# A weight matrix stored piece by piece, so that one transfer of 2 KB runs brings each piece

## The chip, the cores and the metric

The kernel runs on one core of a Trainium2 chip, as one program. The metric is the device time of a whole execution in microseconds; lower is better. Packing of inputs on the host before the launch isn't in it.

## The reference, cut to what matters

Two blocks of a network are computed for 256 tokens of 1024 channels. The first has a recurrent mixer and a layer that looks up rows of two tables (PEER): each token picks 16 of 16384 experts in each of 8 heads, and so uses 128 rows of table u and 128 of table v. The second block has a pooling layer and an attention layer, each followed by a gated feed-forward network (FFN) on the 256 latent tokens; the first FFN is also applied to 256 context tokens. What matters here is that FFN:

```python
def _conv_ffn(h, w_up, conv_w, conv_b, w_down):
    u = h @ w_up                       # (256, 1024) @ (1024, 5632), float32
    up = jnp.pad(u, ((0, 0), (1, 1), (0, 0)))
    u = up[:, :-2] * conv_w[0] + up[:, 1:-1] * conv_w[1] + up[:, 2:] * conv_w[2] + conv_b
    a, v = jnp.split(u, 2, axis=-1)    # columns 0..2815 and 2816..5631
    return (jax.nn.silu(a) * v) @ w_down
```

Column c of the first half is always used together with column 2816 + c of the second.

## The kernel before

All is float32. Weights stream through a ring of three slots of 128 partitions x 4096 floats (2 MB each), written by DMAs that SyncE (SP) issues in program order (`load`, L540). A load waits until the slot's last reader is done, issues its transfers, and notes the semaphore value that means "landed". `weights` (L660) makes TensorE wait for that value.

The up matrix is used in 11 pieces of 256 + 256 columns. `up` (L563) gives two transfers for a piece: for each of the 128 partitions and 8 blocks of 128 rows, 256 columns of the first half, and the same of the second half. In memory a row of the matrix is 5632 floats, so that each transfer consists of 1024 runs of 1 KB; in the slot a block's two runs lie beside each other. `down` (L568) gives one transfer a load, with runs of 512 columns, 2 KB. The 11 up pieces are loaded three times: by the loop at L605 for the context tokens (layer 0), and twice by `ffn_loads` (L617), for the latent tokens in layers 0 and 1. That makes 66 transfers.

The work around them differs:

- From about 330 to 1130 us the PEER rows are fetched. GpSimd (POOL, L2723) issues 512 indirect DMAs, *gathers*, each bringing one row of 4 KB into each of 128 partitions (0.524 MB), 256 from table u and 256 from table v, into a ring of 12 places. A gather waits until the place's last reader is done: VectorE (L1802) multiplies a u row with the tokens; TensorE multiplies v rows in pairs. The order is fixed by `ROWS` and `turns` (L379). Into TensorE's part of it `woven` (L431) sets the context work as steps: every few gathers in that order, one half step of the context's FFN (8 matmuls of 128x128 by 128x256, 16 weight loads in the trace). So TensorE meets up pieces and v rows in an order written out beforehand, and waits at whichever isn't there. Of the context's up pieces the first three are loaded from 432 us on, the others from 608 us on as the slots become free; the six down loads follow from 772 us.
- From about 1145 us the latent FFNs run. There each piece is first split into a high and a low part (ScalarE L2133, VectorE L1419), which frees its slot, and TensorE makes three passes of the parts (`mm3`). Between the two FFNs lies the attention layer.

Of the kernel before, what the change touches and what calls it, by code (L numbers as in the profile page):

```python
# [60 lines left out]
def packed_vectors(x):  # L61
    def cols(v):
        return np.reshape(v, (-1, 128)).T

    small = np.concatenate([np.reshape(x[n][0], -1) for n in
                            ("gdn_dt_bias", "gdn_a_log", "mlstm_i_bias", "mlstm_f_bias")])
    convw = np.transpose(np.reshape(x["conv_w"][0], (12, 128, 5)), (1, 0, 2)).reshape(128, 60)
    parts = [cols(x["norm1_g"][0]), cols(x["mlstm_norm_g"][0]), cols(x["gdn_norm_g"][0]), cols(x["attn_q_gain_2"][0]),
             cols(x["attn_k_gain_2"][0]), cols(x["c_2"][0]), cols(x["c_ctx_2"]),
             cols(x["pool_b_2"][0]), cols(x["pool_scale_2"][0]), cols(x["norm_w_2"]), cols(x["ada_b_2"]),  # L70
             cols(x["ffn_conv_w_2"]), cols(x["ffn_conv_b_2"]), convw, np.broadcast_to(small, (128, 32))]
    return np.ascontiguousarray(np.concatenate(parts, 1))


def packed_ada(w):

    w = np.reshape(w, (2, 4, 2, 128, 3, 4, 512))
    return np.ascontiguousarray(np.transpose(w, (0, 4, 1, 3, 2, 5, 6)).reshape(24, 128, 4096))


def packed_gates(w):

    g = np.concatenate([w[:, 2048:2064], w[:, 4112:4128]], 1)
    g = np.transpose(np.reshape(g, (8, 128, 32)), (1, 0, 2)).reshape(128, 256)
    return np.ascontiguousarray(np.concatenate([g, np.tile(np.eye(32, dtype=np.float32), (4, 1))], 1))


def packed_keys(k):
# [3 lines left out]
def program(nc, a, out):  # L92
# [32 lines left out]
    def at(name, n):  # L125

        sem = S[name]
        while name in GOES_ON:
            name, before = GOES_ON[name]
            n += before  # L130
        return sem, n

    def sb(name, n, stack=ctx, p=128):
        return stack.enter_context(nc.sbuf_tensor(name, [p, n], F32))
# [18 lines left out]
    vec = sb("vec", NVEC)  # L153
# [121 lines left out]
    bands = [(hpC[:, 392 * g:392 * g + 256], hpC[:, 392 * g + 256:392 * g + 392]) for g in range(4)]  # L275
# [208 lines left out]
    def split_done(n):  # L484

        if n in (34, 40, 41):
            return "g_lo", (34, 40, 41).index(n) + 1
        return "v_lo", n + 1 - sum(n > m for m in (34, 40, 41))
# [48 lines left out]
    def _(sp):  # L537
        free, count, nth = [None] * 4, [0] * 4, [0]

        def load(name, until, *parts, n=4, slot=None):  # L540

            i = nth[0] % n if slot is None else slot
            nth[0] += 1
            for signal in free[i] or ():
                sp.wait_ge(*at(*signal))
            for put, src in parts:
                sp.dma_start(put(slots[i]), src).then_inc(S[f"d_w{i}"], 16)
                count[i] += 16
            free[i] = until if isinstance(until, list) else [until]
            ready[name] = S[f"d_w{i}"], count[i], slots[i]  # L550
# [6 lines left out]
            return ((lambda ap: ap[:, 0:2048].rearrange("p (g c) -> p g c", g=8)),  # L557
                    a["pool_w_2"][0].rearrange("g (k p) c -> p (g k) c", p=128))

        def up_part(i):  # L560
            return lambda ap: ap.rearrange("p (k i c) -> p k i c", k=8, i=2)[:, :, i, :]

        def up(l, g):  # L563
            w = a["ffn_w_up_2"][l]
            return ((up_part(0), w[:, 256 * g:256 * g + 256].rearrange("(k p) c -> p k c", p=128)),
                    (up_part(1), w[:, 2816 + 256 * g:3072 + 256 * g].rearrange("(k p) c -> p k c", p=128)))

        def down(l, half, f0, nf):  # L568
            w = a["ffn_w_down_2"][l]
            return ((lambda ap: ap[:, 0:512 * nf].rearrange("p (f c) -> p f c", f=nf)),  # L570
                    w[128 * f0:128 * (f0 + nf), 512 * half:512 * half + 512].rearrange("(f p) c -> p f c", p=128))
# [30 lines left out]
        sp.dma_start(cl[:, 0:1536], a["c_late"]).then_inc(S["d_l"], 16)  # L602
        load("poolc", ("p_cpl", 4), pool_w(), n=3)
        for g in range(11):
            load(("cup", g), ("p_cu", 2 * g + 2), *up(0, g), n=3)  # L605
        for half in range(2):
            for q, (f0, nf) in enumerate(((0, 8), (8, 8), (16, 6))):
                load(("cdn", half, q), ("p_cd", 4 * (3 * half + q) + 4), down(0, half, f0, nf), n=3)
# [7 lines left out]

        def ffn_loads(l, n0):  # L617
            for g in range(11):
                load(("up", l, g), split_done(n0 + 2 * g + 1), *up(l, g), n=3)
            for half in range(2):  # L620
                for q, (f0, nf) in enumerate(((0, 8), (8, 8), (16, 6))):
                    load(("dn", l, half, q), split_done(n0 + 23 + 6 * half + 2 * q), down(l, half, f0, nf), n=3)

        ffn_loads(0, 0)
        load("kv", [split_done(34), split_done(35)], kcols(a["attn_w_qkv_2"][0], 1024, 512), n=3)
        for q in range(2):
            load(("q", q), split_done(37 + 2 * q), kcols(a["attn_w_qkv_2"][0], 512 * q, 512), n=3)
        for i in range(LOADS_EARLY, 24):
            load(("ada", i), ("p_adb", i - LOADS_EARLY + 1), (lambda ap: ap, a["ada"][i]), n=3)
            if i in (LOADS_EARLY + 5, 23):  # L630
                q = int(i == 23)
                load(("o", q), split_done(41 + 2 * q), kcols(a["attn_w_o_2"][0], 512 * q, 512), n=3)
        ffn_loads(1, 44)
        for n, (q, t) in enumerate(((0, 0), (0, 1), (1, 0), (1, 1))):
            sp.wait_ge(*at("a_yo" if t == 0 else "v_yo", q + 1))
# [6 lines left out]
    def _(pe):  # L642
# [509 lines left out]
        def peer():  # L1152
            for what in turns():
# [8 lines left out]
                elif what[0] == "use" and ROWS[what[1]][0] == "v" and ROWS[what[1]][2] % 2 == 1:  # L1162
                    _, s, m = ROWS[what[1]]
                    if m == 1:
                        pe.wait_ge(*at("v_wT", s + 1))
                        if s == 0:
                            for i in (5, 6):
                                pe.wait_ge(*at(held[i][0], held[i][1]))
                        elif s == 4:
                            pe.wait_ge(*at("v_add", 1))  # L1170
                    for i in range(2):
                        for k in range(m - 1, m + 1):
                            n = NTH["v", s, k]
                            q, c = four_of(k)
                            if i == 0:
                                pe.wait_ge(*at(f"d_r{n % NR}", 16 * (n // NR + 1)))
                            o = mm(vb[i][32 * q:32 * q + 32, :], alone[s % 2][:, q, c, :], ring[n % NR][:, 512 * i:512 * i + 512],
                                   s % 4 == 0 and k < 4, s % 4 == 3 and k > 27)
                            if i == 1:
                                o.then_inc(S["p_v"], 1)  # L1180
                elif what[0] == "window_sums":
                    pe.wait_ge(*at("d_l", 48))
                    for n in range(2):
                        b = take(("zb", n), "a_sz", 1)
                        for e in range(2):
                            mm(b[:, 256 * e:256 * e + 256], ones, bands[2 * n + e][0], e == 0, False)
                            k = mm(b[:, 256 * e + 120:256 * e + 256], ones, bands[2 * n + e][1], False, e == 1)
                    k.then_inc(S["p_zb"], 1)
# [215 lines left out]
    def _(ve):  # L1404
# [357 lines left out]
        def rows(t, step):  # L1762


            y, r = yrows[:, t, :], ss[:, 4 * t + 2:4 * t + 3]
            _, r2, root, s, rs = norm_at(t)
            if step == 0:
                ve.wait_ge(*at("d_g2", 32))
                told(tt(y, x1[:, t, :], nfb, MUL), *rows_at(t, "gain"))
            elif step == 1:  # L1770
                ve.wait_ge(*at("a_ss", 5 + 2 * t))
                seq(ve.reciprocal(r, ss[:, 4 * t + 1:4 * t + 2]))
                told(stt(r2, r, 1.0 / 1024, r, MUL, MUL), *rows_at(t, "root"))
            else:
                ve.wait_ge(*at("a_ss", 6 + 2 * t))
                if t == 0:
                    ve.wait_ge(*at("p_ckv", 3))
                seq(ve.reciprocal(s, root))
                seq(tt(rs, r, s, MUL))
                told(ts(zrows[:, t, :], y, rs, None, MUL, BYP), *rows_at(t, "pool"))  # L1780
                told(ts(y, y, r, None, MUL, BYP), *rows_at(t, "scaled"))

        def peer():
            for what in turns():
# [9 lines left out]
                elif what[0] == "use" and ROWS[what[1]][0] == "u":  # L1794
                    n = what[1]
                    _, t, m = ROWS[n]
                    j, k = 8 * t + m // 16, m % 16
                    if j > 1 and k == 0:
# [851 lines left out]
    def _(po):  # L2650
# [115 lines left out]


_INS = ["x", "w_in", "w_out", "norm2_g", "normf_g", "peer_wq", "peer_u", "peer_v", "ctx_2", "pool_w_2", "attn_w_qkv_2",
        "attn_w_o_2", "ffn_w_up_2", "ffn_w_down_2"]


# [19 lines left out]
```

## Time and profile before

| what | value |
|---|---|
| median of 3 runs | 1712.83 us (1711.22 to 1714.83) |
| the profiled execution | 1713.59 us, span of its instructions 1711.7 us |
| TensorE busy | 88% of the span, mean granted clock 0.94 |
| VectorE, GpSimd, ScalarE busy | 64%, 46%, 32% |
| moved by DMA | 477.24 MB, mean 279 GB/s |
| of these by q0, the gathers | 268.47 MB |
| of these by q1, what SP issues | 207.27 MB |

How to read it: times of stretches are microseconds from the span's start. A line such as L666 is a helper that issues every matmul; tiles tell the groups apart. `ps` is a PSUM bank, `wring` the slots, `arena` the memory that the tables' rows and the activations share, and a few gathers land in the fourth slot and so carry the name `wring` too. PEld is TensorE's loading of weights, which shows best when a matmul started. q0 is the queue of GpSimd's gathers, q1 that of SP's loads; the share in a queue's row is the time of its packets over the 16 DMA engines. That can be over 100% in sum, since packets overlap, so that a share near 1.03 means that the DMA engines had always something to do.

### The profile page before, as it was taken

How to read it: one execution, taken by the hardware profiler on the slowest of the kernel's cores; microseconds unless marked ns; L12 is line 12 of the kernel's file. 1: busy time of each engine (PE TensorE's matmuls, PEld its weight loads, DVE VectorE, ACT ScalarE, POOL GpSimd, SP SyncE). 2: the span in 40 equal slices, each digit the busy share in tenths (PEclk: the TensorE clock that was granted, in tenths of full speed). 3: DMA queues.
4: the chain of work that ended last, by engine and by line, in shares of the span. 5: the costliest groups of instructions: out<-in, count | busy, mean ns of one | idle time of the engine just before them, and what ended most of it. 6: DMA issues, size and time to landing. Idle time of an engine off the chain costs nothing.

```text
span 1711.7 us, 23479 instructions
## 1 busy us (share of the span) xinstructions
PE 1498.0 (88%) x9034; PEld 1109.4 (65%) x9034; DVE 1093.5 (64%) x2121; ACT 554.4 (32%) x782; POOL 790.4 (46%) x746
## 2 busy tenths in 40 slices
PE   7999998775566699999788866989999999999999
PEld 6997676663212266666333432449999985699999
DVE  4865654689489867766856665237775436567753
ACT  6652121211221131322100011236654524466542
POOL 0024230276667765746777777624561101225630
PEclk9999999997878899999999997999999898999999
DMA  7447770498999999999999999985654425746550
GB/s 273 149 148 294 278 278 25 158 398 305 384 398 400 409 396 391 394 382 400 406 404 400 404 371 408 408 307 187 195 185 158 175 105 191 266 130 196 192 178 26
DMA packets 188575, 477.24 MB, mean 279 GB/s; under 512 B 10544, under 2 KB 80432, under 8 KB 185264
## 3 DMA queue, kind: packets, MB, share of 16 engines
q0 software_dynamic: 73728, 268.47, 40.3%
q1 hardware_dynamic: 114736, 207.27, 34.1%
q8 instruction: 72, 1.18, 0.3%
q14 instruction: 39, 0.32, 0.1%
HBM read 474.65 MB, written 1.05 MB: 278 GB/s over the span
## 4 chain that ended last, share of the span: by engine, by line
PE 57%; DMA 15%; DVE 10%; POOL 7%; issue 4%; ACT 1%; DVEq 0%; ACTq 0%; SPq 0%; POOLq 0%
PE ps L666 57%; DMA arena<-in_peer_v,cl 8%; POOL arena L2723 6%; DMA wring<-in_ffn_w_up 3%; DVE arena L1802 2%; DMA wring<-in_peer_v,cl 2%; DVE arena L1419 1%; POOL wring L2723 1%; DMA arena<-in_peer_u,arena 1%; PE ps L670 1%; DVE arena L1425 1%; DMA wring<-in_peer_u,arena 1%; DVE wring L1802 1%; DVE arena L1732 0%; DMA wring<-in_ada 0%
## 5 line engine op out<-in xcount | busy, mean ns | idle before, releaser
L666 PE MATMUL ps<-arena,wring 128*128 128x256 f32 (+2 forms) x2360 | 595.5, 489 | 105.5 <-DMA arena<-in_peer_v,cl 97.4
L666 PEld LDWEIGHTS ps<-arena,wring 128*128 128x128 f32 (+1 forms) x2360 | 330.4, 167 | 352.7 <-DMA arena<-in_peer_v,cl 176.5
L1802 DVE CUSTOM_DVE_ANT_0 arena<-arena 128x1024 f32<-128x1024 f32 x214 | 257.2, 1227 | 124.7 <-DMA arena<-in_peer_u,arena 121.3
L2723 POOL DMA_INDIRECT arena<-in_peer_u,arena x214 | 240.2, 1123 | 198.5 <-DVE arena L1760 80.0
L2723 POOL DMA_INDIRECT arena<-in_peer_v,cl x214 | 222.9, 1042 | 82.4 <-issue 57.9
L2130 ACT ACT_TABLE_LOAD x64 | 82.1, 1283 | 388.1 <-DVE arena L1802 266.9
L1419 DVE TENSOR_TENSOR wl<-wring,wh 128x2048 fp32r<-128x2048 f32 (+1 forms) x76 | 167.8, 2208 | 60.7 <-ACT wh L2133 58.6
L666 PE MATMUL ps<-hh,wh 128*128 128x256 f32 x704 | 201.2, 286 | 3.9 <-DVE hl L1425 3.9
L666 PE MATMUL ps<-hl,wh 128*128 128x256 f32 x704 | 200.8, 285 | 0.0
L666 PE MATMUL ps<-hh,wl 128*128 128x256 f32 x704 | 200.7, 285 | 0.0
L1425 DVE SCALAR_TENSOR_TENSOR cvb<-ps,vec,cvb 128x255 f32<-128x255 f32 x264 | 127.5, 483 | 106.9 <-ACT cvb L2130 99.6
L2133 ACT ACTIVATE wh<-wring 128x2048 fp32r<-128x2048 f32 x78 | 146.1, 1873 | 76.5 <-PE ps L666 74.7
L2741 POOL TENSOR_TENSOR cvb<-cvb 128x256 f32<-128x256 f32 x44 | 97.2, 2210 | 106.5 <-ACT cvb L2130 106.5
L666 PEld LDWEIGHTS ps<-arena 128*128 128x128 f32 (+1 forms) x868 | 103.7, 193 | 56.1 <-issue 28.6
L666 PEld LDWEIGHTS ps<-hh,wh 128*128 128x128 f32 x704 | 136.8, 194 | 4.3 <-issue 4.3
L666 PEld LDWEIGHTS ps<-hl,wh 128*128 128x128 f32 x704 | 136.9, 194 | 0.0
L666 PEld LDWEIGHTS ps<-hh,wl 128*128 128x128 f32 x704 | 136.8, 194 | 0.0
L666 PE MATMUL ps<-arena 128*128 128x128 f32 (+4 forms) x868 | 117.0, 294 | 19.7 <-ACT arena L2133 10.8
L2130 ACT ACTIVATE cvb<-ps,vec 128x256 f32<-128x256 f32 x132 | 74.6, 565 | 178.2 <-PE ps L666 174.5
L2677 POOL TENSOR_TENSOR arena<-arena,cl 128x256 f32<-128x256 f32 x56 | 43.0, 768 | 167.4 <-PE ps L666 164.2
L666 PE MATMUL ps<-ah,wh 128*128 128x256 f32 x352 | 99.6, 283 | 0.0
L666 PE MATMUL ps<-al,wh 128*128 128x256 f32 x352 | 99.6, 283 | 0.0
(261 smaller groups left out, 2324.0 us busy)
## 6 DMA issues: line engine op xcount, KB each, us to landing
wring<-in_ffn_w_up SPq DMA_DIRECT2D x66, 1024.0 KB, 8.3
wring<-in_ada SPq DMA_DIRECT2D x24, 2048.0 KB, 8.7
wring<-in_ffn_w_down SPq DMA_DIRECT2D x12, 2048.0 KB, 8.4
wring<-in_w_in SPq DMA_DIRECT2D x8, 2048.0 KB, 8.1
wring<-in_ffn_w_down SPq DMA_DIRECT2D x6, 1536.0 KB, 7.9
wring<-in_peer_wq SPq DMA_DIRECT2D x4, 2048.0 KB, 20.7
wring<-in_attn_w_qkv SPq DMA_DIRECT2D x4, 2048.0 KB, 9.0
wring<-in_w_out SPq DMA_DIRECT2D x2, 2048.0 KB, 8.2
```

Source lines behind the costliest of these rows:

```text
L666: return pe.matmul(o, l, r, start=start, stop=stop)
L670: return pe.transpose(o, i, ident[0:n, 0:n])
L1419: return ve.tensor_tensor(o, x, y, op)
L1425: return ve.scalar_tensor_tensor(o, x, s, y, op0, op1)
L1802: ve.tensor_tensor_reduce(out=o, in0=o, in1=h2[:, t, :], scale=1.0, scalar=0.0, op0=MUL, op1=ADD, accum_out=dots[j % 2][:, k:k + 1]).then_ ...
L2130: return ac.activation(o, x, f, bias=bias, scale=scale, accum_out=accum)
L2133: return ac.activation(o, x, ACT.Copy)
L2677: k = po.tensor_tensor(OTs[l % 2][:, m:m + 2, :], AM[:, m:m + 2, :], bc(cl[:, o:o + 128], 2, 1), MUL)
L2723: po.indirect_dma_start(out=ring[n % NR], out_offset=None, in_=table, in_offset=bass.IndirectOffsetOnAxis(ap=which, axis=0)).then_inc(S[f" ...
L2741: seq(po.tensor_tensor(cv[:, 0, :], cv[:, 0, :], cv[:, 1, :], MUL))
```

## The change

The host packs the up matrices of both layers into a new input, `ups`, of shape (2 layers, 11 pieces, 8 blocks, 128 rows, 512): a row of a piece has its 256 columns of the first half and its 256 of the second beside each other. A load is one transfer from it, with 1024 runs of 2 KB, and raises its semaphore by 16 where the pair raised it by 32. What lies in the slot is the same as before; order, slots and waits are the same too. A piece is one region of 2 MB in memory: partitions 2 KB apart, blocks 256 KB apart.

```diff
+def packed_up(w):
+
+    return np.ascontiguousarray(np.transpose(np.reshape(w, (2, 8, 128, 2, 11, 256)), (0, 4, 1, 2, 3, 5)).reshape(2, 11, 8, 128, 512))
...
-        def up_part(i):
-            return lambda ap: ap.rearrange("p (k i c) -> p k i c", k=8, i=2)[:, :, i, :]
-
         def up(l, g):
-            w = a["ffn_w_up_2"][l]
-            return ((up_part(0), w[:, 256 * g:256 * g + 256].rearrange("(k p) c -> p k c", p=128)),
-                    (up_part(1), w[:, 2816 + 256 * g:3072 + 256 * g].rearrange("(k p) c -> p k c", p=128)))
+            return (lambda ap: ap.rearrange("p (k x) -> p k x", k=8)), a["ups"][l, g].rearrange("k p x -> p k x")
...
-            load(("cup", g), ("p_cu", 2 * g + 2), *up(0, g), n=3)
+            load(("cup", g), ("p_cu", 2 * g + 2), up(0, g), n=3)
...
-                load(("up", l, g), split_done(n0 + 2 * g + 1), *up(l, g), n=3)
+                load(("up", l, g), split_done(n0 + 2 * g + 1), up(l, g), n=3)
```

The input `ffn_w_up_2` is no longer passed to the chip.

## Rows read from the trace of the kernel before

**Rows 1.** The page's parts 1, 3 and 6: engines, DMA queues, the matrix's loads

```profile
PE 1498.0 (88%) x9034; PEld 1109.4 (65%) x9034; DVE 1093.5 (64%) x2121; ACT 554.4 (32%) x782; POOL 790.4 (46%) x746
...
wring<-in_ffn_w_up SPq DMA_DIRECT2D x66, 1024.0 KB, 8.3
```

**Rows 2.** The table by stretches: us, busy (x) by engine, PEclk, DMA share, GB/s

```profile
596.00:725.00 129.00, 128.45 (x581) 87.31 (x579) 97.94 (x233) 31.58 (x53) 84.09 (x78) 1.00 1.04 394
...
733.00:736.00 3.00, 3.00 (x8) 2.37 (x7) 1.71 (x4) 0.00 (x0) 0.00 (x0) 0.50 1.04 396
...
825.00:975.00 150.00, 128.50 (x483) 63.42 (x483) 99.11 (x239) 9.55 (x15) 111.46 (x104) 0.97 1.03 405
975.00:1025.00 50.00, 37.94 (x147) 18.60 (x146) 35.21 (x86) 4.17 (x6) 39.11 (x36) 0.95 0.99 374
1160.00:1350.00 190.00, 189.84 (x1570) 189.87 (x1571) 120.17 (x135) 106.05 (x117) 81.47 (x71) 0.99 0.55 184
```

**Rows 3.** The chain that ended last, 590 to 830: start us, us, what

```profile
596.28 90.09 PE ps L666 x400
...
686.79 44.34 DMA wring<-in_ffn_w_up
```

**Rows 4.** Waits of PE, 596 to 811: us, times, longest

```profile
PE ps L666 <- DMA wring<-in_ffn_w_up: 6.3, 1, 6.3
```

**Rows 5.** PEld in order of time, 720 to 760: start us, us

```profile
721.19 3.32 PEld L666 LDWEIGHTS ps<-arena,wring 128*128 128x128 f32 x16 [0.84 <-issue]
731.18 6.03 PEld L666 LDWEIGHTS ps<-arena,wring 128*128 128x128 f32 x16 [6.67 <-DMA wring<-in_ffn_w_up]
737.54 0.14 PEld L666 LDWEIGHTS ps<-arena,wring 128*32 128x32 f32 x4 [0.33 <-issue]
...
744.87 6.77 PEld L666 LDWEIGHTS ps<-arena,wring 128*128 128x128 f32 x32 [0.84 <-issue]
751.97 0.14 PEld L666 LDWEIGHTS ps<-arena,wring 128*32 128x32 f32 x4 [0.33 <-issue]
```

**Rows 6.** POOL's gathers that waited for PE, in order of time

```profile
625.22 0.94 POOL L2723 DMA_INDIRECT wring<-in_peer_u,arena  x1 [2.67 <-PE ps L666]
...
639.66 0.94 POOL L2723 DMA_INDIRECT arena<-in_peer_u,arena  x1 [2.55 <-PE ps L666]
...
740.22 0.94 POOL L2723 DMA_INDIRECT arena<-in_peer_u,arena  x1 [9.44 <-PE ps L666]
```

**Rows 7.** DMA from 465 to 485, gathers beside 1 KB runs: packets, MB, share

```profile
q0 software_dynamic: 1701, 6.19, 79.5%
q1 hardware_dynamic: 1704, 1.71, 24.4%
```

**Rows 8.** DMA from 560 to 590, gathers alone

```profile
q0 software_dynamic: 3375, 12.29, 102.9%
```

**Rows 9.** DMA from 856 to 868, gathers beside 2 KB runs (w_down)

```profile
q0 software_dynamic: 806, 2.94, 62.4%
q1 hardware_dynamic: 913, 1.87, 41.0%
```

**Rows 10.** DMA from 731 to 757, all queues

```profile
DMA packets 5356, 9.81 MB, mean 377 GB/s; under 512 B 249, under 2 KB 3869, under 8 KB 5355
```

**Rows 11.** DMA issues, 686 to 688, then 772 to 773: KB, us to landing

```profile
wring<-in_ffn_w_up SPq DMA_DIRECT2D x2, 1024.0 KB, 38.1
...
wring<-in_ffn_w_down SPq DMA_DIRECT2D x1, 2048.0 KB, 24.4
```

**Rows 12.** Waits of POOL, 825 to 1050

```profile
POOL arena L2723 <- PE ps L666: 7.1, 14, 1.4
POOL wring L2723 <- PE ps L666: 6.9, 4, 3.3
```

**Rows 13.** DMA from 596 to 686, then from 825 to 975, the q1 rows

```profile
q1 hardware_dynamic: 7297, 7.36, 23.5%
...
q1 hardware_dynamic: 2864, 5.77, 10.2%
```

More of the change, by code:

```diff
@@ L2768 @@
 _INS = ["x", "w_in", "w_out", "norm2_g", "normf_g", "peer_wq", "peer_u", "peer_v", "ctx_2", "pool_w_2", "attn_w_qkv_2",
-        "attn_w_o_2", "ffn_w_up_2", "ffn_w_down_2"]
+        "attn_w_o_2", "ffn_w_down_2"]
 def kernel(**inputs):
@@ L2780 @@
     given = {n: x[n] for n in _INS}
-    given |= {"ada": packed_ada(x["ada_w_2"]), "c_base": base, "c_levels": levels, "c_late": late, "c_bands": bands, "vec": packed_vectors(x),
+    given |= {"ups": packed_up(x["ffn_w_up_2"]), "ada": packed_ada(x["ada_w_2"]), "c_base": base, "c_levels": levels, "c_late": late, "c_bands": bands, "vec": packed_vectors(x),
               "gates": packed_gates(x["w_in"][0]), "keys": packed_keys(x["peer_keys"][0])}
```

## The prediction

> **What bounds the kernel now.** I read the page first: 66 transfers of 1 MB from the up matrix [rows 1]. TensorE is busy for 88% of the span, but that is a mean over stages, so the table by stretches comes next [rows 2]. Two thirds of the up loads feed the latent FFNs. From 1160 to 1350 TensorE is busy for 189.84 of 190 us at clock 0.99 and the DMA engines for 55%: loads are hidden there. The other third, 11 pieces, feeds the context's FFN beside the gathers. From 596 to 725 TensorE is busy for 128.45 of 129 us and DMA's share is 1.04, at 394 GB/s: both are full. From 825 on DMA is full too (405 GB/s), but for 975 to 1025 (374 GB/s). The chain of waits says what gives way [rows 3]: TensorE's work for 90.09 us, then a load of an up piece, 44.34 us long, then TensorE again. In TensorE's waits this load is the only DMA that it waits for between 596 and 811, 6.3 us once [rows 4].
>
> **What that stall costs.** In TensorE's weight loads a whole step is 16 + 16 loads in 6.77 us, and the v rows behind it begin 7.10 us after its start (744.87 to 751.97). The step cut in two by the stall starts at 721.19, and its v rows at 737.54, so 16.35 us later [rows 5]. The stall costs 16.35 - 7.10 = 9.25 us, and not 6.3: behind the wait 16 weight loads take 6.03 us, before it 3.32. The table shows why: the granted clock is 0.50 from 733 to 736, the lower level of 1.2 GHz, after TensorE has idled [rows 2].
>
> **Why the load was late.** GpSimd, held back by TensorE, issues eight gathers in 639.66 - 625.22 = 14.44 us [rows 6], 1.8 us each. The order sets a step every 5.6 gathers (L431), two steps for a piece: 11.2 gathers, 20.2 us. So at TensorE's pace gathers need 8 x 0.524 / 14.44 = 290 GB/s, and a piece of 2.10 MB has to come every 20.2 us, 104 GB/s: 394 in all.
> With 1 KB runs beside gathers, q1 moves 1.71 MB in 20 us, 85.5 GB/s, and q0 6.19 MB, 309.5 GB/s [rows 7]. The two queues take about as many packets each (1704 and 1701), so bytes go by packet size. A piece takes 2.10 / 85.5 = 24.5 us, over 4 us more than the period. Each load falls further behind, to a median of 38.1 us to landing for the two transfers issued at 686 [rows 11], and the last of it at 731.1 [rows 3].
>
> **The change, part by part.**
> *Packets of 2 KB beside gathers.* The down loads show them: from 856 to 868 q1 moves 1.87 MB in 12 us, 156 GB/s, and q0 2.94 MB, 245 GB/s [rows 9]. A piece takes 2.10 / 156 = 13.5 us. That is under 20.2 us, so no backlog builds up; a piece may take 44.3 - 6.3 = 38 us from its issue before TensorE misses it [rows 3, 4]. A down load issued at 772, in the same mix and with TensorE still busy, took 24.4 us [rows 11]. I take the stall as gone: -9.25 us on TensorE's chain.
> *Gathers get less while a load runs.* 245 GB/s for 13.5 us and 410 (12.29 MB in 30 us [rows 8]) for the other 6.7 us make a mean of 300, against 290 needed. That just suffices.
> *DMA's own work.* While a 1 KB piece loads, gathers lose (410 - 309.5) / 410 of 24.5 us, 6.0 us; while a 2 KB piece loads, (410 - 245) / 410 of 13.5 us, 5.4 us. The saving is 0.59 us a piece, for 11 pieces 6.5 us. The packets' own time gives a lower value: 0.235 x 16 x 90 us / 7297 = 46.4 ns for 1 KB, 0.102 x 16 x 150 / 2864 = 85.5 ns for 2 KB [rows 13]; 7.3 ns a pair, for 11264 pairs over 16 engines 5.1 us.
> The Trainium skill (DMA: Bandwidth & Descriptors, "Why small descriptors are slow (HBM only)") speaks against this: a packet costs 3 cycles on top of one for each 32 bytes, and joining is said to pay only up to 256 bytes. By that, two packets of 32 + 3 cycles become one of 64 + 3, 4.3% less, and this term would be about 2.8 us, an estimate from that page. The trace has a larger effect, 8% (92.8 to 85.5 ns), and the sum goes by the trace.
> *Three early pieces* are loaded between 432 and 558 us, beside gathers that TensorE waits for. Their share of the saving, 3 x 0.59 = 1.8 us, comes before 596 and adds to the 9.25.
> *Issues.* 33 fewer transfers for SP. SP waits for slots, and nothing is queued behind a load but the next one. In the context's stage a pair's second issue is held up by the backlog, and that ends with it. I cost it at nothing; what it is worth is in the stall.
> *The 22 latent pieces.* They are hidden by TensorE (DMA share 0.55, above): nothing. Without that cover they would bring a gain too, since the same bytes come sooner. At 1124 the first two are issued behind the last gathers, pool_w's 1 MB ahead of them; ScalarE reads the first at 1146. Nothing again; taking share from the last few gathers could cost 1 us at most.
>
> **The sum.** TensorE's chain gives 9.25 + 1.8 = 11.0 us by 811. Whether this arrives at 1125 depends on DMA: it was full all the while, so the total of its work can't end earlier than that work shrinks. That is 6.5 us, and the gap behind the stall, where GpSimd had nothing to issue for 9.44 us [rows 6] and DMA fell to 377 GB/s for 26 us [rows 10], 18 under the 395 of 1 KB runs beside gathers [rows 7]: 26 x 18 / 395 = 1.2 us. So DMA's bound is 7.7 us. GpSimd bounds it as well: from 825 to 1050 it waits for TensorE's release 18 times, 14.0 us in all [rows 12]; the rest is its own pace, which passes the whole 11.0 on, as does the stretch at 374 GB/s, where DMA could catch up by 50 x (1 - 374/410) = 4.4 us. Between 7.7 and 11.0 I take 7.7, because 825 to 975 runs at 405 GB/s, next to the 410 of gathers alone. The profiled execution took 1713.59 us, 0.76 over the median: 1705.9 for it, 1705.1 against the median of 1712.83. A measurement of this kernel can tell about 0.2%, 3.4 us, from no change.
>
> **The rivals.**
> *The whole chain arrives* (18%). DMA keeps up and catches up at 975 to 1025; the gain is 11.0, the time 1701.8. For it: GpSimd hardly waits in that stretch. Against: the DMA rate there.
> *The wait only moves* (17%). Packets of the new matrix cost as much a byte as before, because all 16 engines read one region of 2 MB with blocks 256 KB apart, which no row shows. The down matrix, with its own regular rows, speaks against it. Then DMA's bound leaves the 1.2 us of the gap: 1711.6. TensorE waits for a v row instead of a piece.
> *Slower* (8%). Gathers fall from 309.5 to 245 GB/s while a load runs, and 12 places are used up in 12 x 0.524 / 245 = 25.7 us, where TensorE's pace asks for 12 x 1.8 = 21.7. A stretch of two loads end to end makes TensorE wait for a v row, up to 4 us, and each wait is followed by a half step at the lower clock, 2.7 us. That is 6.7 us for each; from two such waits on, the gain is gone, and three of them give 1712.8 - 7.7 + 20 = 1725. Against it: the two down loads at 772 and 791 are 20 us apart beside busy TensorE, and no wait for a gather stands in TensorE's waits before 811 [rows 4].
> *The runs stay at 1 KB* (2%), if the transfer is cut otherwise than the down loads: 1712.8.
>
> **How the numbers follow.** The forecast has the remaining 55%, with its own range from 5.1 us (the packets' own time, the gap not closed) to 11.0: 1701.8 to 1707.7. The range takes in the whole-chain case with 1.8 us more, should the clock of other stretches gain too: 1700.0. Upward it takes in most of the case of the moved wait: 1711.8. Outside stay the slower case and its like. Faster by over 0.2% (below 1709.4): 55 + 18, and a third of the moved-wait case, 78%. Within: 14%. Slower: 8%.
>
> **What would show it.** In the changed trace the up loads are 33 transfers of 2048 KB; beside gathers q1 runs near 156 GB/s and q0 near 245; landing falls from 38 to 15 to 25 us; PE has no wait for an up piece between 596 and 811, PEclk stays at 1.00 there, and this stretch ends 9 to 11 us earlier. At 1125 the shift is still 7 to 11 us, and after 1160 it doesn't change. I am wrong if PE waits for v rows there instead, if q1's 2 KB packets take over 90 ns, or if the shift at 811 shrinks below 3 us by 1125.

## The result, and the profile after

The changed kernel takes 1710.37 us, the kernel before 1714.84 us on the same chip (medians of 20 runs each). The ratio is 0.998, with a 95% interval of 0.9971 to 0.9990, so 1.7 to 5.0 us less. The difference of the medians is 4.5 us, and the ratio itself stands for 3.4. Three more measurements of the same changed kernel, told below, gave 0.9962, 0.9963 and 0.9974. Weighted by the inverse squares of their intervals' widths the four make 0.9975, 4.3 us. The forecast was a gain of 7.7 us. The sign came; of the size this measurement's ratio gives under half (3.4 us), the four together a little over half.

The page's parts 1, 3 and 6 of the changed kernel; its profiled execution took 1709.29 us, 4.30 less than that of before:

```profile
span 1707.4 us, 23446 instructions
...
PE 1502.6 (88%) x9034; PEld 1113.6 (65%) x9034; DVE 1093.1 (64%) x2121; ACT 554.4 (32%) x782; POOL 797.2 (47%) x746
...
wring<-in_ups SPq DMA_DIRECT2D x33, 2048.0 KB, 10.7
```

33 transfers of 2048 KB stand where [rows 1] had 66 of 1024 KB. No engine's busy time falls by more than 0.4 us: the gain is in waiting. The table by stretches, columns as in [rows 2]:

```profile
596.00:725.00 129.00, 128.99 (x587) 86.40 (x586) 97.31 (x231) 31.58 (x53) 82.19 (x76) 1.00 1.02 398
...
730.00:745.00 15.00, 15.00 (x68) 10.20 (x68) 13.83 (x38) 2.07 (x4) 8.87 (x9) 1.00 1.03 402
...
825.00:975.00 150.00, 129.13 (x481) 63.24 (x481) 98.25 (x234) 9.55 (x15) 107.92 (x102) 0.94 1.03 404
975.00:1025.00 50.00, 35.07 (x135) 16.50 (x134) 33.76 (x85) 5.09 (x6) 39.28 (x36) 0.91 1.00 389
```

The clock of 0.50 is gone, and so is the stall. TensorE's waits for other engines and DMAs from 596 to 811 (us, times, longest), against [rows 4]:

```profile
PE ps L666 <- DMA arena<-in_peer_v,cl: 2.2, 2, 1.2
```

TensorE's weight loads in order of time (start us, us), against [rows 5]:

```profile
719.25 3.32 PEld L666 LDWEIGHTS ps<-arena,wring 128*128 128x128 f32 x16 [0.84 <-issue]
...
724.75 6.77 PEld L666 LDWEIGHTS ps<-arena,wring 128*128 128x128 f32 x32 [0.84 <-issue]
731.85 0.14 PEld L666 LDWEIGHTS ps<-arena,wring 128*32 128x32 f32 x4 [0.33 <-issue]
```

The step takes 6.77 us with its v rows 7.10 us after its start, the undisturbed value. The two queues from 618 to 624, beside each other in the stage that mattered (packets, MB, share):

```profile
q0 software_dynamic: 426, 1.56, 64.5%
q1 hardware_dynamic: 429, 0.88, 38.1%
```

That is 260 GB/s for the gathers and 147 for the load; 245 and 156 were forecast from [rows 9]. Taken over a whole load the rate is lower: the packets of one piece spread over 14.9 to 16.4 us of the trace, 128 to 141 GB/s, where 13.5 us were forecast. The five up loads issued between 604 and 700 land after a median of 19.7 us; ten transfers of before took 32.4 in the same window.

So the stall and the load behind it went as forecast, at somewhat lower rates. One sign failed in this profile already: the stretch was to end 9 to 11 us earlier, and gather 288, issued near its end, comes 5.5 us earlier (below). The rest of what didn't come is seen in the chain that ended last (start us, us, what), against [rows 3]:

```profile
599.83 102.50 PE ps L666 x464
...
702.44 7.79 PE ps L666 x32
...
710.57 81.49 PE ps L666 x366
...
803.12 15.74 DMA arena<-in_peer_v,cl
...
826.75 11.84 DMA arena<-in_peer_v,cl
```

TensorE's work now runs from 599.83 to 792, and then the chain passes to gathers of v rows. The gathers issued from 768 to 792 (KB left out by the view; the last number is us to landing), first in the kernel before:

```profile
arena<-in_peer_u,arena POOLq DMA_INDIRECT x8, 8.8
arena<-in_peer_v,cl POOLq DMA_INDIRECT x3, 9.3
```

and in the changed kernel:

```profile
arena<-in_peer_u,arena POOLq DMA_INDIRECT x6, 15.4
arena<-in_peer_v,cl POOLq DMA_INDIRECT x6, 15.6
```

The stall had held up GpSimd too ([rows 6]), and so DMA's queue of gathers had run short. Without the stall it is nearly twice as long in time (15.4 and 15.6 us to landing against 8.8 and 9.3). Waits for gathers from 785 to 870 (us, times, longest), before:

```profile
PEld ps L666 <- DMA arena<-in_peer_v,cl: 9.1, 6, 3.6
...
DVE arena L1802 <- DMA arena<-in_peer_u,arena: 7.2, 5, 2.3
```

after:

```profile
DVE arena L1802 <- DMA arena<-in_peer_u,arena: 16.5, 10, 5.8
...
PEld ps L666 <- DMA arena<-in_peer_v,cl: 14.6, 10, 3.6
```

**Progress by gather.** To see what is given back, the kernels have to be compared at the same point of the work, not at the same time. The 512 gathers are issued in one fixed order, so the time between the issues of gather m and gather n, counted from 0, is such a ruler. It is worked out from GpSimd's instructions in each profiled execution. The three early up loads fall in 64 to 144, the stall of before in 208 to 288.

```
kernel (runs of the context's up loads)  64-96  64-144  208-288  288-368
before (1 KB)                             48.8   125.8    147.1    121.0
changed kernel (2 KB)                     52.9   127.6    138.1    124.6
```

The stall's 9.0 us are there, and 3.6 of them are gone again 80 gathers later. At gather 208 the changed kernel is 3.5 us behind (661.3 against 657.8), at 288 5.5 ahead, at 368 1.9 ahead, at 511 3.7 ahead (1121.6 against 1125.3). The experiments' tables lean on the columns above, which agree within 2 to 5 us among kernels of a kind; from 64 to 208 the spread is larger (224.7 to 230.2 us in the four kernels with early runs of 1 KB). From 368 to 511 the time goes with the chip more than with the kernel: 197.6 to 200.6 us in the five profiles from chips where the kernel before takes 1713 to 1715 us, 205.4 to 213.2 in the twelve from chips where it takes 1725 to 1727, with DMA at 396 to 402 GB/s in three of the first and 385 to 390 in three of the others. Effects of 3 to 4 us can't be followed through that stretch across chips.

### The profile page after: what moved, and what is told of

It is laid out like the page before. It is cut to its first block, busy times and chain, and to the rows that moved or that the text cites. A ratio compares the mean times of both kernels' runs of the same rounds, so it can differ in the third digit from the quotient of the medians.

```text
span 1707.4 us, 23446 instructions
## 1 busy us (share of the span) xinstructions
PE 1502.6 (88%) x9034; PEld 1113.6 (65%) x9034; DVE 1093.1 (64%) x2121; ACT 554.4 (32%) x782; POOL 797.2 (47%) x746
## 4 chain that ended last, share of the span: by engine, by line
PE 59%; DMA 12%; DVE 9%; POOL 9%; issue 4%; ACT 1%; DVEq 0%; ACTq 0%; POOLq 0%
PE ps L666 59%; DMA arena<-in_peer_v,cl 9%; POOL arena L2723 7%; DVE arena L1802 2%; DMA wring<-in_peer_v,cl 2%; POOL wring L2723 1%; DVE arena L1419 1%; DVE arena L1425 1%; PE ps L670 1%; DMA wring<-in_peer_u,arena 1%; DMA wring<-in_ada 1%; DVE wring L1802 0%; DVE arena L1732 0%; DVE pr L1422 0%; DVE arena L1422 0%
## 5 line engine op out<-in xcount | busy, mean ns | idle before, releaser
L666 PE MATMUL ps<-arena,wring 128*128 128x256 f32 (+2 forms) x2360 | 600.1, 491 | 103.2 <-DMA arena<-in_peer_v,cl 97.7
L666 PEld LDWEIGHTS ps<-arena,wring 128*128 128x128 f32 (+1 forms) x2360 | 332.0, 167 | 352.6 <-DMA arena<-in_peer_v,cl 175.5
L2723 POOL DMA_INDIRECT arena<-in_peer_u,arena x214 | 240.8, 1125 | 190.9 <-DVE arena L1760 79.3
L2723 POOL DMA_INDIRECT arena<-in_peer_v,cl x214 | 226.7, 1059 | 78.9 <-issue 58.2
L666 PE MATMUL ps<-hh,wh 128*128 128x256 f32 x704 | 202.1, 287 | 3.9 <-DVE hl L1425 3.9
L666 PE MATMUL ps<-hl,wh 128*128 128x256 f32 x704 | 201.6, 286 | 0.0
L666 PE MATMUL ps<-hh,wl 128*128 128x256 f32 x704 | 201.6, 286 | 0.0
L666 PEld LDWEIGHTS ps<-hh,wh 128*128 128x128 f32 x704 | 137.7, 196 | 4.4 <-issue 4.4
L666 PEld LDWEIGHTS ps<-arena 128*128 128x128 f32 (+1 forms) x868 | 103.7, 193 | 56.1 <-issue 28.6
L666 PEld LDWEIGHTS ps<-hl,wh 128*128 128x128 f32 x704 | 137.8, 196 | 0.0
L666 PEld LDWEIGHTS ps<-hh,wl 128*128 128x128 f32 x704 | 137.7, 196 | 0.0
L666 PE MATMUL ps<-arena 128*128 128x128 f32 (+4 forms) x868 | 117.0, 294 | 19.7 <-ACT arena L2133 10.8
L666 PE MATMUL ps<-ah,wh 128*128 128x256 f32 x352 | 99.6, 283 | 0.0
L666 PE MATMUL ps<-ah,wl 128*128 128x256 f32 x352 | 99.6, 283 | 0.0
## 6 DMA issues: line engine op xcount, KB each, us to landing
wring<-in_peer_wq SPq DMA_DIRECT2D x4, 2048.0 KB, 14.6
```

The costliest lines, as they stand in the source:

```text
L666: return pe.matmul(o, l, r, start=start, stop=stop)
L2723: po.indirect_dma_start(out=ring[n % NR], out_offset=None, in_=table, in_offset=bass.IndirectOffsetOnAxis(ap=which, axis=0)).then_inc(S[f" ...
```

## The experiments

Four questions: which of the 33 loads matter; whether it is the runs or the layout in memory; whether DMA's work takes the rest of the gain back; and what becomes of the three early pieces. Where it stands, `up_old` is the pair of transfers of before, from the matrix of before. Medians are compared with the kernel before on the same chip. An edit moves the line numbers: L674, L671 and L668 below are the matmul helper that was L666.

### The changed kernel again

No edit.

> The changed kernel once more, for a second profile. Theory A (DMA takes back what TensorE gains): the stretch at TensorE's pace ends about 9 us sooner after its own start than before, and 3 to 5 us of that are given back before 860, as waits of TensorE and VectorE for gathers; in all 3 to 5 us faster than before. Theory B (the profile taken was an unlucky one): the 9 us are kept to 1125, in all 8 to 11 us faster. The slow patch of DMA at 515 to 535 returns if it belongs to the change, and is elsewhere or absent if it doesn't.

1720.18 against 1725.07 us, ratio 0.9962 (0.9942 to 0.9983). This chip is 10 us slower for both kernels; only ratios and differences go from one chip to another. By the ruler it repeats the stall's end and the give-back, 138.1 us from 208 to 288 and 126.8 from 288 to 368 (first of the three repeats in the table of the early pieces).

### New loads for the context alone

```diff
-                load(("up", l, g), split_done(n0 + 2 * g + 1), up(l, g), n=3)
+                load(("up", l, g), split_done(n0 + 2 * g + 1), *up_old(l, g), n=3)
```

> Only the context's 11 pieces come from the packed matrix in 2 KB runs, the 22 latent pieces as before. Both theories: as the changed kernel, 0.998 of before within 0.001 (3 to 5 us faster), because the latent FFNs hide their loads. If the latent pieces had a part: closer to 1.

1722.36 us, 0.9981 (0.9957 to 1.0005). By the ruler it is the changed kernel: 138.5 us from 208 to 288, 123.9 from 288 to 368. The only DMAs that TensorE waits for from 596 to 811 are v rows:

```profile
PE ps L674 <- DMA arena<-in_peer_v,cl: 2.2, 2, 1.2
```

### New loads for the latent FFNs alone

```diff
-            load(("cup", g), ("p_cu", 2 * g + 2), up(0, g), n=3)
+            load(("cup", g), ("p_cu", 2 * g + 2), *up_old(0, g), n=3)
```

> Only the 22 latent pieces come from the packed matrix, the context's as before. Theory A and B: no difference, within 1 us of before, and the stall of some 6 us for a context piece near 725 is back. A rival, that the latent stages or the last gathers at 1125 pay for or gain from the larger packets: 2 us or more either way.

1723.97 us, 0.9988 (0.9968 to 1.0007), nothing that can be told from none. The stall is back, 146.8 us from 208 to 288; TensorE's waits for DMAs from 596 to 830:

```profile
PE ps L674 <- DMA wring<-in_ffn_w_up: 7.2, 2, 6.4
```

With the run for the context alone, this places the gain in the context's 11 loads as far as the profiles go. The two ratios differ by less than their intervals and don't show it by themselves.

### The new layout with runs of 1 KB

```diff
+        def up_halves(l, g):
+            def part(i):
+                return lambda ap: ap.rearrange("p (k i c) -> p k i c", k=8, i=2)[:, :, i, :]
+            return tuple((part(i), a["ups"][l, g][:, :, 256 * i:256 * i + 256].rearrange("k p x -> p k x")) for i in range(2))
...
-            load(("cup", g), ("p_cu", 2 * g + 2), up(0, g), n=3)
+            load(("cup", g), ("p_cu", 2 * g + 2), *up_halves(0, g), n=3)
...
-                load(("up", l, g), split_done(n0 + 2 * g + 1), up(l, g), n=3)
+                load(("up", l, g), split_done(n0 + 2 * g + 1), *up_halves(l, g), n=3)
```

> The packed matrix, but each piece in two transfers with runs of 1 KB, as before: layout in memory alone. If the length of the run is the cause (A and B): as before, within 1 us, q1 near 85 GB/s beside gathers, the stall near 725 there. If the nearness of the data in memory is the cause: the gain of the changed kernel, 3 to 5 us.

1726.22 us, 1.0002 (0.9979 to 1.0024). The queues from 465 to 485 are those of [rows 7], and TensorE's wait from 596 to 830 is the old one:

```profile
q0 software_dynamic: 1700, 6.19, 79.6%
q1 hardware_dynamic: 1698, 1.71, 24.3%
```

```profile
PE ps L671 <- DMA wring<-in_ups: 6.1, 2, 4.6
```

Where the bytes lie in memory does nothing that can be measured here. The stall goes with the length of the runs. This run also has 66 transfers again, as the kernel before had; no run separates their number from the length of their runs in time. For the rates the trace does: the down loads of before are single transfers with 2 KB runs and had 156 GB/s, and the same 33 transfers with longer runs, below, have 210 and 353.

### Half the bytes in the late loads

This run leaves out half of the up matrix's rows for the context's pieces from the fourth on; the matmuls are all still done.

```diff
-            load(("cup", g), ("p_cu", 2 * g + 2), up(0, g), n=3)
+            load(("cup", g), ("p_cu", 2 * g + 2), up(0, g) if g < 3 else
+                 ((lambda ap: ap[:, 0:2048].rearrange("p (k x) -> p k x", k=4)), a["ups"][0, g, 0:4].rearrange("k p x -> p k x")), n=3)
```

> The changed kernel, but of the last eight context pieces only the first four of eight blocks are loaded (the other half of a slot keeps old numbers, so the context's values are others). This takes about 8 x 2.7 = 21 us of work from DMA, from 612 us on. Theory A (TensorE's pace bounds the stage, the changed kernel then gives back about 5 us because its gathers land later): the stage ends 9 us sooner as in the changed kernel, hardly anything is given back, and the whole is 8 to 12 us faster than before, 0.993 to 0.995. Theory C (DMA's work bounds the whole stretch from 596 to 1125): about 20 us or more beyond the changed kernel, 0.986 or less.

1717.38 against 1727.25 us, 0.9953 (0.9931 to 0.9974): 8.1 us less than before (4.5 to 11.9), where the changed kernel has 4.3 less. The intervals of the two overlap, so that this difference rests on the ruler more than on the times. From 208 to 288 it takes 137.9 us, like the changed kernel. From 288 to 368 it takes 119.0, where six profiles with late runs of 2 KB took 122.5 to 126.8: nothing is given back, in one profile. That speaks for DMA's work as what takes the gain back. 8.4 MB fewer would be 21 us at 400 GB/s, and only some 4 us of them reach the end; without the debt another pace is the bound, as the forecast had it with TensorE's chain. The table from 596 to 811 shows DMA no longer pressed, 373 GB/s:

```profile
596.00:811.00 215.00, 206.98 (x944) 139.55 (x936) 162.84 (x390) 55.72 (x93) 139.51 (x128) 0.99 0.99 373
```

### New loads for the three early pieces alone, and for the eight late ones alone

```diff
-            load(("cup", g), ("p_cu", 2 * g + 2), up(0, g), n=3)
+            load(("cup", g), ("p_cu", 2 * g + 2), *((up(0, g),) if g < 3 else up_old(0, g)), n=3)
```

The second kernel has `g > 2` in place of `g < 3`; both keep `up_old` for the latent FFNs.

> Only the three context pieces loaded between 432 and 558 us come in 2 KB runs, all others as before. The prediction gave them 1.8 us. Theory A: nothing (1.000 within the interval), since GpSimd's pace between 505 and 545 takes the lead away: DMA falls to 300 to 360 GB/s there and gather 128 is issued at the same time as in the kernel before, within 1.5 us. The stall near 725 stays.

> Only the context's last eight pieces come in 2 KB runs. Theory A: the whole effect of the change, 3 to 6 us (0.9965 to 0.998), with no load stall between 596 and 811. If the early three carry part of it: less than the changed kernel by 2 us.

Early: 1725.73 us, 1.0010 (0.9989 to 1.0031). Late: 1721.07 us, 0.9970 (0.9947 to 0.9994). The eight late pieces carry the gain. Waits of TensorE from 596 to 815 in the first,

```profile
PE ps L674 <- DMA wring<-in_ffn_w_up: 5.2, 2, 4.3
```

and in the second:

```profile
PE ps L674 <- DMA arena<-in_peer_v,cl: 2.3, 3, 1.1
```

The early pieces show in the first column of the ruler:

```
kernel                        64-96  64-144  208-288  288-368
new latent loads alone (1 KB)  48.6   128.6    146.8    122.1
new layout, 1 KB runs          48.0   127.2    146.8    121.0
late eight new (early 1 KB)    47.8   126.9    137.5    125.6
early three new (late 1 KB)    52.8   128.3    144.2    123.7
context alone new (2 KB)       52.2   129.1    138.5    123.9
changed kernel, three repeats  52.3   126.5    138.1    126.8
                               53.6   126.5    139.5    122.5
                               53.4   129.8    137.3    126.0
```

With early runs of 2 KB gather 96 comes 4 to 5 us later: the loads take from the gathers, at a time when the loads are in no hurry and the gathers are. By gather 144 this is made up: 125.8 to 128.6 us with 1 KB, 126.5 to 129.8 with 2 KB. So the saved DMA work isn't lost to another load, it is just not used. From 510 to 540, before and then after:

```profile
510.00:540.00 30.00, 21.35 (x67) 6.36 (x65) 28.93 (x66) 1.50 (x2) 23.00 (x20) 0.94 1.03 404
```

```profile
510.00:540.00 30.00, 17.32 (x55) 6.37 (x55) 28.93 (x65) 1.42 (x2) 24.52 (x19) 0.81 0.94 351
```

VectorE is busy for 28.93 of 30 us in both. GpSimd is full as well: 19 gathers take it 24.52 us, each issue follows the one before after 0.30 us, and some issues take 1.99 us that take 0.94 elsewhere. The chain that ended last runs over it in the changed kernel:

```profile
512.54 1.99 POOL arena L2723
...
536.17 1.99 POOL arena L2723
```

So the pace of GpSimd and VectorE is the bound there, and not DMA, which falls to 351 GB/s; which of the two engines sets it, no run separates. The ruler says the same more broadly: from gather 112 to 144 all 17 profiles took 47.2 to 50.8 us, whether DMA moved 362 GB/s meanwhile or 412. Nor is the drop a mark of the new loads by itself: with early runs of 1 KB the stretch from 510 to 540 had 356 to 404 GB/s, with 2 KB 333 to 363.

### Longer runs: 4 KB and 16 KB

Two, or all eight, of a piece's blocks are packed beside each other for each partition. Here is the kernel with 16 KB; the other has 4 and 2 for 1 and 8.

```diff
-... .reshape(2, 11, 8, 128, 512))
+... .reshape(2, 11, 1, 8, 128, 512).transpose(0, 1, 2, 4, 3, 5).reshape(2, 11, 1, 128, 4096))
...
-            return (lambda ap: ap.rearrange("p (k x) -> p k x", k=8)), a["ups"][l, g].rearrange("k p x -> p k x")
+            return (lambda ap: ap.rearrange("p (k x) -> p k x", k=1)), a["ups"][l, g].rearrange("k p x -> p k x")
```

> All pieces in runs of 4 KB (two blocks beside each other in memory), the slot as before. Packets as large as the gathers' own: beside gathers q1 and q0 should each get about 200 GB/s, a piece takes 10 to 11 us, and DMA's work for a piece falls from 5.4 to about 5.1 us. Theory A: no wait for a load, debt to gathers 2 us smaller than in the changed kernel, 0 to 3 us faster than it. A rival: gathers with half the rate for 10 us make TensorE wait within the stage, and it is slower than the changed kernel.

> All pieces in runs of 16 KB, one for each partition. If DMA takes turns by packet, q1 gets about 320 GB/s beside gathers and q0 some 80 while a piece loads (7 us), unless a packet is cut. Theory A: gathers landing 5 us later each time, made good within the period, so as the changed kernel within 3 us; a rival, that such a hole of 7 us makes TensorE wait for a v row at each of the eight pieces, each followed by the lower clock: 10 us or more slower than before.

4 KB: 1721.78 us, 0.9981 (0.9958 to 1.0004). 16 KB: 1719.56 us, 0.9963 (0.9940 to 0.9987). Neither can be told from the changed kernel (0.9963 on the chip of the 16 KB run; it was not run on that of the 4 KB run). The queues, for 4 KB from 620 to 624, and for 16 KB from 641 to 644:

```profile
q0 software_dynamic: 228, 0.84, 51.5%
q1 hardware_dynamic: 206, 0.84, 51.2%
```

```profile
q1 hardware_dynamic: 65, 1.06, 83.7%
q0 software_dynamic: 60, 0.22, 18.1%
```

In the middle of a load the queues take about as many packets each at every length: 1704 to 1701 at 1 KB, 429 to 426 at 2 KB, 206 to 228 at 4 KB, 65 to 60 at 16 KB. So the load's rate beside gathers is 85.5, 147, 210 and 353 GB/s at 1, 2, 4 and 16 KB. The Trainium skill (DMA: Bandwidth & Descriptors, "Queues, rings and completion order") states that each DMA engine takes turns between its queues packet by packet, a packet being some 9 to 17 descriptors. The equal counts here agree with turns of equally many runs; how many runs make a turn they don't show. At 16 KB gathers keep 73 GB/s, and gather 96 is 8 us later than with 1 KB (56.2 us); but a late load is over sooner (its packets spread over 6.3 to 8.2 us of the trace, and behind the middle of a load gathers get more than one packet for one), and its one profile took 118.6 us from 288 to 368, as with half the bytes. With 4 KB one profile kept only some 3.5 us up to gather 368 (142.1 + 122.5 against 268.2), less than with 2 KB, so that single profiles don't put the lengths in order. The time at the end shows no more of this than its interval of 4 us lets through.

### The early loads spread out

If early loads hurt by pressing on the gathers all at once, they should be spaced. The first three wait until TensorE has used 32, 40 and 56 of the 256 gathers of v rows. It is tried with 2 KB runs, with the kernel before (1 KB), and with 16 KB runs.

```diff
+            if g < 3:
+                sp.wait_ge(*at("p_v", (32, 40, 56)[g]))
```

> The changed kernel, but its first three context pieces are issued later: after 32, 40 and 56 of the v rows are used (about 508, 526 and 577 us) instead of at 432. Theory A: the early loads in 2 KB runs take rate from gathers that TensorE and VectorE wait for (gather 96 was issued some 4 us later than with 1 KB runs), and DMA then stands partly idle at 515 to 540; issued there, they are nearly free. Gather 96 is issued 5 us or more sooner than in the changed kernel, and the whole is 2 to 6 us faster than it. A rival, that the stretch up to 596 is bound by the pace of GpSimd and VectorE anyway: gather 96 is sooner, gather 144 and the end aren't, within 1 us.

> The kernel before with the same delay of the first three context pieces. Their loads then take 24 us each beside gathers; the third is issued at 577 and has some 45 us. Theory A: 0 to 4 us faster than before; the stall of a later piece stays, and could come sooner since all eight others queue behind.

> The changed kernel for a third time, beside the staggered one on the same chip. Theory A: 0.996 to 0.998 of before; from gather 208 to gather 368 some 5 us less than in the kernel before, of 9 us less from 208 to 288.

One chip: spaced with 2 KB 1717.18 us, 0.9953 (0.9934 to 0.9973); the kernel before, spaced, 1722.12 us, 0.9990 (0.9971 to 1.0010); the changed kernel 1719.73 us, 0.9963 (0.9943 to 0.9984).

> Runs of 16 KB for all pieces, and the first three context pieces delayed to 32, 40 and 56 used v rows. If the two effects are separate (the early loads' timing, worth 7 us up to gather 144; and DMA's debt after the stage, 6 us less with 16 KB runs from gather 208 to 368), they add up: 0.990 to 0.994 of before, 4 us or more faster than the staggered kernel with 2 KB runs. If what is saved early is lost at the next stretch that GpSimd and VectorE bound: as the staggered kernel within 2 us.

> The staggered kernel with 2 KB runs again, for a closer figure: 0.994 to 0.9965 of before; from gather 64 to gather 144 about 7 us less than in the changed kernel.

> The changed kernel a fourth time on the chip of the two others: 0.9965 to 0.998, so 2 to 5 us slower than the staggered one if the 7 us are partly kept.

Another chip: spaced with 16 KB 1704.81 us, 0.9933 (0.9913 to 0.9952); with 2 KB 1707.73 us, 0.9957 (0.9941 to 0.9973); the changed kernel 1711.67 us, 0.9974 (0.9957 to 0.9991).

```
kernel                          64-96  64-144  208-288  288-368
before, spaced (1 KB)            46.8   118.9    149.5    122.2
spaced, 2 KB, first chip         46.1   119.9    142.2    121.5
spaced, 2 KB, second chip        45.4   120.1    139.3    126.7
spaced, 16 KB                    45.0   118.3    137.9    122.1
half the bytes (late, 2 KB)      53.2   129.0    137.9    119.0
4 KB                             56.0   129.6    142.1    122.5
16 KB                            56.2   129.0    137.9    118.6
```

Spacing wins some 8 to 11 us up to gather 144, in all four profiles that have it (118.3 to 120.1, where 125.8 to 129.8 stood without). The kernel before keeps none of it that can be measured: its stall is still there (7.7 us of waits from 596 to 815) and grows from 147 to 149.5 us.

```profile
PE ps L668 <- DMA wring<-in_ffn_w_up: 7.7, 3, 4.4
```

With 2 KB runs, where the only DMAs waited for in that window are v rows,

```profile
PE ps L668 <- DMA arena<-in_peer_v,cl: 1.6, 2, 1.0
```

a part arrives: the ratio is lower than the changed kernel's by 0.0010 on one chip and 0.0017 on the other, 2 to 3 us, which the intervals don't separate. With 16 KB runs the end is 11.5 us earlier than the kernel before by the ratio (0.67% of 1715.11) and 10.3 by the medians, the best of all that ran; it is clear of the changed kernel beside it (0.9974, 0.9957 to 0.9991), but not of the spaced one with 2 KB, from which 4 us or more were expected and 2.9 came by the medians. Its rows from 505 to 540 and from 596 to 811,

```profile
505.00:540.00 35.00, 22.12 (x64) 6.48 (x58) 33.02 (x78) 4.87 (x6) 28.01 (x22) 0.78 1.02 412
...
596.00:811.00 215.00, 207.72 (x934) 139.40 (x935) 163.88 (x390) 55.68 (x93) 130.78 (x124) 0.99 1.02 409
```

beside the changed kernel's from 505 to 540:

```profile
505.00:540.00 35.00, 22.32 (x77) 9.02 (x76) 33.65 (x76) 1.42 (x2) 27.74 (x21) 0.83 0.95 359
```

DMA moves 412 GB/s where it moved 359, because loads lie where GpSimd and VectorE are the bound, and then 409 GB/s over the full stage. The reading is that spacing uses DMA's spare time and long runs cut its work behind. That both parts are needed isn't shown: spacing alone and 16 KB alone were each within their intervals of the changed kernel.

## Why the prediction was right, and where it was wrong

The mechanism came, and its size was wrong. The sum had 7.7 us, made of 6.5 us of DMA's saved work for 11 pieces and 1.2 us for the gap behind the stall; about 4.3 arrived. The term that failed for certain is the share of the three early pieces, 3 x 0.59 = 1.8 us of the 6.5; whether the other 1.2 us came stays open.

**The stall: right.** "The stall costs 16.35 - 7.10 = 9.25 us" and is gone. From 208 to 288 the four kernels with late runs of 1 KB and no spacing took 146.2 us on average (before, new latent loads alone, new layout, early three), the six with 2 KB 138.2 (the changed kernel four times, context alone, late eight): 8.0 us less. The new layout with 1 KB runs keeps the stall, so that the layout isn't what removes it.

**DMA's bound on the late pieces: right, as far as the profiles tell.** From 288 to 368 the same kernels take 122.0 and 124.9 us, so 2.9 of the 8.0 us are given back and 5.1 are kept. The forecast's step for this is 0.59 us of DMA work saved a piece; for the eight late pieces 4.7. That it comes so near 5.1 is partly luck: with the changed kernel's own rates, 147 and 260 GB/s, the same step gives 6.0 - 5.2 = 0.8 us a piece and 6.3 for eight, and the packets' own time (46.4 and 85.8 ns) gives 3.6. Half the bytes, which lifts that bound, kept 11.3 us to gather 368 (137.9 + 119.0 against 146.2 + 122.0), in one profile, and the forecast had 9.25 to 11.0 for TensorE's chain alone. The Trainium skill's 4.3% a pair ("Why small descriptors are slow (HBM only)" in DMA: Bandwidth & Descriptors) would have saved 2.8 / 11 = 0.25 us a piece, an estimate from that page, 2.0 for eight. The trace doesn't agree: a 2 KB packet took 0.241 x 16 x 90 / 4047 = 85.8 ns in the changed kernel from 596 to 686, in the row below, against 46.4 for 1 KB [rows 13], 7.5% less than two of those.

```profile
q1 hardware_dynamic: 4047, 8.18, 24.1%
```

**The three early pieces: wrong.** The step that failed is the one that took the saving of 0.59 us for all 11 pieces, and with it "Their share of the saving, 3 x 0.59 = 1.8 us, comes before 596 and adds to the 9.25". Measured: 1.0010 (0.9989 to 1.0031) for those three alone, and 0.9970 for the eight without them. By itself the first interval still reaches a gain of 1.9 us; the ruler settles it, for by gather 144 nothing of a saving is left (128.1 us on average with 2 KB, 127.1 with 1 KB). I had looked at one stretch beside those loads (465 to 485, where DMA was full) and taken the whole time to gather 144 for DMA-bound. From 510 to 540 it was the pace of GpSimd and VectorE that bound it, and what DMA saved before was idle time there.

**The gap behind the stall: not seen.** "26 x 18 / 395 = 1.2 us" was to be added to DMA's bound. Kept to gather 368 are 5.1 us, so there is room for 0.4 beside the 4.7; but the profiles' differences, up to 4 us within a group, can't settle a term of this size. What is left of the sum, 6.5 + 1.2 less 1.8 and 1.2, is 4.7, and 4.3 us are measured.

**Signs.** Of those set down, the transfers' count and size, the landing, PEclk and the end of the wait for an up piece came as said, the rates nearly (147 and 260 GB/s for 156 and 245). A sign of being wrong was that TensorE waits for v rows there instead: it does, for 2.2 us in place of 6.3. "At 1125 the shift is still 7 to 11 us" failed: 3.7 us. The shift near 811 (gather 288) was 5.5 us and not 9 to 11, since in the one profile of each 3.5 us were lost before 596, which is why it had to be read by gathers.

**The rivals.** The whole chain's arrival (11.0 us) is excluded by the interval; half the bytes, 8.1 us (4.5 to 11.9), speaks for it coming had DMA not been behind. The wait that only moves had a price of 1.2 us, by packets that cost as much a byte as before, which their time excludes (85.8 ns against twice 46.4), as the 1 KB runs on that layout show no cost of it (1.0002); yet its picture, TensorE waiting for v rows instead of pieces, is what took place for the part given back. The slower rival's mechanism showed as well, 14.6 us of waits for v rows from 785 to 870 against 9.1, the longest 3.6 us in both; but they came in a stage where TensorE isn't full, and did not add up to its price. The latent pieces are worth nothing that can be measured, as costed.

## What to carry to other kernels

Where two queues shared full DMA engines here, the length of a queue's runs set its share (85.5 to 353 GB/s for the loads, from 1 to 16 KB), so longer runs are a priority as well as a saving: give them to loads that are late, and keep them out of the way of what is more urgent. Removing a wait in a stage where another resource is full too was worth about what that resource's work shrank by, 5 us of 8; cost the saving stage by stage, and count it only where that resource is the bound. Compare traces by a fixed order of instructions, since a gain that is given back is not to be seen at equal times.

## What was not expected of the hardware

In the middle of a load runs of 16 KB go out one for each row of 4 KB: 65 packets to 60, a load at 353 GB/s and gathers at 73. Length goes on paying for the packets' own time: 46.4 ns for 1 KB, 85.8 for 2 KB, 0.512 x 16 x 4000 / 206 = 159 ns for 4 KB, and 0.837 x 16 x 3000 / 65 = 618 ns for 16 KB, or 46, 43, 40 and 39 ns a KB. DMA's busy share was 0.99 with 373 GB/s in the run with half the bytes, and 1.02 with 409 in the best one: near 1 the share doesn't say how much more could be moved. And executions of one kernel here spread over 11.5 us (1706.31 to 1717.85 in 20 runs) where the effect is 4.3: one execution's time shows nothing of that size, and neither does a profile from gather 368 to 511, where the chips differ by some 8 us.
